# Recurrence, compression and attention of one mixer in another order (fp32 block pair, one core)

## What is computed

```python
def mixer_ab(h, w_in, conv_w, conv_b, w_r, b_r, w_i, b_i, lam, pe_k, pe_v, wk1, wk2, wv1, wv2, w_out):
    xr, gr, q, kc, vc, ks, vs, kw, vw, gl = jnp.split(h @ w_in, splits, axis=-1)
    y_rnn = rg_lru(causal_dwconv(xr, conv_w, conv_b), w_r, b_r, w_i, b_i, lam) * jax.nn.gelu(gr)
    y_att = nsa(q, kc, vc, ks, vs, kw, vw, gl, pe_k, pe_v, wk1, wk2, wv1, wv2)
    return jnp.concatenate([y_rnn, y_att], axis=-1) @ w_out
# rg_lru:  r, i = sigmoid(x @ w_r + b_r), sigmoid(x @ w_i + b_i)     (block diagonal)
#          log_a = -8 r softplus(-lam);  h_t = exp(log_a) h_{t-1} + sqrt(-expm1(2 log_a)) (i x)
```

## Time and profile before

| | us |
|---|---|
| median of three runs | 2596.81 |
| the profiled execution | 2601.1 |
| its span in the trace | 2597.6 |
| TensorE busy | 2420.9 (93%) |
| VectorE busy | 1654.0 (64%) |
| ScalarE busy | 1183.4 (46%) |
| mean granted TensorE clock | 0.93 of 2.4 GHz |

### The profile page before, as it was taken

How to read it: one execution, slowest core, us unless ns; L and a number is a source line. 1 busy time by engine, 2 the same in 40 slices (tenths; PEclk the granted TensorE clock), 3 DMA queues, 4 the chain that set the end, 5 groups by cost and what they waited for, 6 DMA issues and landing times.

```text
span 2597.6 us, 47292 instructions
## 1 busy us (share of the span) xinstructions
PE 2420.9 (93%) x18874; PEld 2299.5 (89%) x18874; DVE 1654.0 (64%) x2637; ACT 1183.4 (46%) x1720; POOL 50.7 (2%) x100
## 2 busy tenths in 40 slices
PE   7999999989997999999989999897799899897997
PEld 7999989879996999989978998797677799797997
DVE  5556889655554555888846555576543676666766
ACT  5444434544443444443544444344243456444654
POOL 0000000000001000000000000000000000000000
PEclk9999999989998999999989999896655899998999
DMA  6556454346556556545245555452200355353552
GB/s 250 179 185 223 150 177 137 110 157 212 185 179 202 186 185 200 194 146 173 97 141 190 192 182 198 159 162 74 81 1 9 111 181 186 114 179 99 186 185 96
DMA packets 110420, 405.90 MB, mean 156 GB/s; under 512 B 12256, under 2 KB 12384, under 8 KB 109920
## 3 DMA queue, kind: packets, MB, share of 16 engines
q1 hardware_dynamic: 96192, 352.33, 40.4%
q0 software_dynamic: 13824, 50.34, 5.6%
q10 hardware_dynamic: 288, 1.57, 0.2%
HBM read 403.14 MB, written 1.05 MB: 156 GB/s over the span
## 4 chain that ended last, share of the span: by engine, by line
PE 87%; DVE 8%; DMA 2%; ACT 2%; issue 1%; POOL 0%; DVEq 0%; SPq 0%; ACTq 0%
PE bank L482 85%; DMA mod_w_buf<-mod_w 2%; PE bank L622 2%; DVE w_lo L1349 1%; DVE arena L1509 1%; DVE work L1418 1%; DVE arena L1756 0%; ACT w_hi L1010 0%; DVE rinv L1383 0%; DVE work L1386 0%; ACT work L1169 0%; DVE rinv L1415 0%; POOL mod_w_buf L471 0%; DVE h_lo L1377 0%; ACT rinv L1031 0%
## 5 line engine op out<-in xcount | busy, mean ns | idle before, releaser
L482 PE MATMUL bank<-h_hi,w_hi 128*128 128x256 f32 (+1 forms) x4016 | 1172.3, 293 | 66.6 <-DVE h_lo L1644 18.2
L482 PE MATMUL bank<-h_hi,w_lo 128*128 128x256 f32 (+1 forms) x4016 | 1152.7, 288 | 0.0
L482 PE MATMUL bank<-h_lo,w_hi 128*128 128x256 f32 (+1 forms) x4016 | 1121.7, 285 | 0.0
L1349 DVE TENSOR_TENSOR w_lo<-w_raw,w_hi 128x1024 fp32r<-128x1024 f32 x663 | 809.2, 1223 | 488.5 <-ACT w_hi L1010 488.2
L1010 ACT ACTIVATE w_hi<-w_raw 128x1024 fp32r<-128x1024 f32 x663 | 699.2, 1056 | 734.1 <-PE bank L482 728.5
L482 PEld LDWEIGHTS bank<-h_hi,w_hi 128*128 128x128 f32 x4016 | 791.9, 197 | 95.5 <-issue 48.5
L482 PEld LDWEIGHTS bank<-h_hi,w_lo 128*128 128x128 f32 x4016 | 791.8, 197 | 0.0
L482 PEld LDWEIGHTS bank<-h_lo,w_hi 128*128 128x128 f32 x4016 | 771.0, 195 | 4.4 <-issue 4.3
L482 PE MATMUL bank<-hid_hi,w_hi 128*128 128x256 f32 x1056 | 299.2, 283 | 2.3 <-DVE hid_lo L1434 2.3
L482 PE MATMUL bank<-hid_lo,w_hi 128*128 128x256 f32 x1056 | 298.8, 283 | 0.0
L482 PE MATMUL bank<-hid_hi,w_lo 128*128 128x256 f32 x1056 | 298.8, 283 | 0.0
(11 more groups left out here) (205 smaller groups left out, 1857.1 us busy)
## 6 DMA issues: line engine op xcount, KB each, us to landing
w_raw<-weights SPq DMA_DIRECT2D x663, 512.0 KB, 3.3
mod_w_buf<-mod_w POOLq DMA_DIRECT2D x96, 512.0 KB, 4.9
tabs<-shape_tables SPq DMA_DIRECT2D x1, 1748.0 KB, 15.8
work<-v_bias ACTq DMA_DIRECT2D x2, 768.0 KB, 4.4
x<-x_fm SPq DMA_DIRECT2D x1, 1024.0 KB, 4.7
out_fm<-x SPq DMA_DIRECT2D x1, 1024.0 KB, 3.9
vecs<-vectors SPq DMA_DIRECT2D x1, 712.0 KB, 7.5
tabs<-shape_tables SPq DMA_DIRECT2D x1, 65.0 KB, 4.7
```

What stands on the lines that cost most here:

```text
L482: ins = pe.matmul(o, lhs, rhs, start=start, stop=stop, skip_group_check=share)
L1349: v.tensor_tensor(w_lo[:, n % SPLIT, :], w_raw[:, n % RAW, :], w_hi[:, n % SPLIT, :].bitcast(F32), ALU.subtract).then_inc(lo_ready[n % SPL ...
```

## The change

Memory: the operands of the r and i gates move to the two-slot buffers `hid_hi` and `hid_lo` (made larger), as does the compression operand, one kind at a time. The attention's buffers move to `kcs` and to the buffer of the first block's modulation weights. The steps `a_exp` and `amp` take the place of `den` and of the square root in `work`.

```diff
+RNN_UNITS = (10, 12, 14, 16, 18, 20, 22, 24)
...
-pct = work_row[:, 0:512]
-scc = work_row[:, 512:512 + NSA_HEADS * N_CMP].rearrange("p (a b) -> p a b", a=NSA_HEADS)
...
+amp = gg
+pt2 = mod_w_row[:, 0:1024].rearrange("p (a b) -> p a b", a=2)
...
 rtmp = work_row[:, 1024:2048].rearrange("p (a b) -> p a b", a=2)
-y2t = it.rearrange("p a b -> p (a b)").rearrange("p (a b) -> p a b", a=TT)
```

```diff
-for i in range(2):
-    column_pair()
-    q_rotated(2 + i)
+column_pair()
+q_rotated(2)
+column_pair()
+q_rotated(3)
 pe.wait_ge(kcs_ready, w.next(kcs_ready))
-for i in range(4):
-    column_pair()
-    if i == 1:
-        k_rotated(0)
-    if i == 3:
-        pe.wait_ge(kr_ready, w.next(kr_ready))
-        k_rotated(1)
-for i in range(2):
-    token_pair()
-branch_gates()
-pe.wait_ge(xc_ready, w.next(xc_ready))
 r_slot = slot()
 i_slot = slot()
 for m in range(KT):
     b = pair_bank()
-    product(half(b, 0), r_slot, m, h_hi[:, m, :], h_lo[:, m, :], True, True)
-    product(half(b, 1), i_slot, m, h_hi[:, m, :], h_lo[:, m, :], True, True, pair_full)
+    pe.wait_ge(xc_ready, w.next(xc_ready))
+    product(half(b, 0), r_slot, m, hid_hi[:, m % 2, :], hid_lo[:, m % 2, :], True, True)
+    if m == KT - 1:
+        slot_done()
+    product(half(b, 1), i_slot, m, hid_hi[:, m % 2, :], hid_lo[:, m % 2, :], True, True, pair_full)
+    if m == KT // 2:
+        k_rotated(0)
 slot_done()
-pe.wait_ge(kcs_split, w.next(kcs_split))
-b = pair_bank(hv_ready)
+branch_gates()
+pe.wait_ge(kr_ready, w.next(kr_ready))
+k_rotated(1)
+for i in range(2):
+    token_pair()
+pe.wait_ge(kr_ready, w.next(kr_ready))
 for kind in range(2):
+    pe.wait_ge(kcs_split, w.next(kcs_split))
     for t in range(2):
         n = slot()
         at = kind * SEQ + t * NSA_KV
...
+            product(bank[3][:, at:at + (N_CMP + 1) * NSA_KV], n, k,
+                    op_hi[:, :, pairs].rearrange("p g n -> p n g"),
+                    op_lo[:, :, pairs].rearrange("p g n -> p n g"),
+                    (kind, t, k) == (0, 0, 0), last, cmp_sum_full if last else None, share=True)
         slot_done()
+    column_pair()
...
-for i in range(KT // 2):
-    column_pair(yrnn_ready if i == 0 else None)
...
+    column_pair()
     pe.wait_ge(cp_ready, w.next(cp_ready))
...
         scores(u)
+    if u in RNN_UNITS:
+        k = RNN_UNITS.index(u)
+        if k % 2 == 0:
+            rnn_bank = pair_bank()
+        column(half(rnn_bank, k % 2), None if k else yrnn_ready, pair_full if k % 2 else None)
     if 1 <= u <= nsa_units:
         turns(u - 1)
```

```diff
+xc_high(0)
+xc_high(1)
 state["tile"] += 1
 for m in range(KT):
     b, free = next_pair(0)
+    if m + 2 < KT:
+        xc_high(m + 2)
     act_f(th[:, m, :], half(b, 0), ACT.Sigmoid, bias=vec("b_r", 0, m)).then_inc(act_link, 1)
...
+operand_high(0)
+b, free = next_pair(1)
+act_f(glog, two(bank[b][:, :])[:, :, 0:3 * NSA_HEADS], ACT.Sigmoid).then_inc(free, 1)
 act.wait_ge(act_link, w.next(act_link, KT))
 act.wait_ge(decay_ready, w.next(decay_ready))
+high_parts(state["tile"] + 2)
+for m in range(KT):
+    ins = act_f(a_exp[:, m, :], th[:, m, :], ACT.Exp, scale=tiny[:, 0, m:m + 1])
+ins.then_inc(act_link, 1)
+b, free = next_pair()
+act_f(vsw[:, 0, :, :], two(bank[b][:, :]), ACT.Copy).then_inc(free, 1)
+act.wait_ge(act_link, w.next(act_link))
 for m in range(KT):
     ins = act_f(th[:, m, :], th[:, m, :], ACT.Tanh, scale=decay[:, m:m + 1])
 ins.then_inc(th_ready, 1)
 act.wait_ge(th_ready, w.next(th_ready))
-act.wait_ge(kr_ready, w.next(kr_ready, 2))
+b, free = next_pair()
+act_f(vsw[:, 1, :, :], two(bank[b][:, :]), ACT.Copy).then_inc(free, 1)
+act_f(amp, th, ACT.Sqrt, scale=-1.0).then_inc(amp_ready, 1)
+state["tile"] += 1
 high_parts(state["tile"] + 1)
-act_f(work[:, :, :], th, ACT.Sqrt, scale=-4.0).then_inc(amp_ready, 1)
-b, _ = next_pair(4)
+state["tile"] += 1
+act.wait_ge(cmp_sum_full, w.next(cmp_sum_full))
+operand_high(1)
...
+gelu_input(0)
+state["tile"] += 1
+high_parts(state["tile"] + 1)
+state["tile"] += 1
+high_parts(state["tile"] + 1)
+act.wait_ge(cmp_sum_full, w.next(cmp_sum_full))
...
+gelu_input(1)
...
+    gelu_input(2 + qt, ACT.Gelu_apprx_tanh if qt else ACT.Copy)
...
+for i in range(0, KT - 2, 2):
+    act_f(gg[:, i:i + 2, :], gg[:, i:i + 2, :], ACT.Gelu_apprx_tanh).then_inc(gelu_ready, 1)
...
+    if 1 <= u <= KT // 2:
+        act.wait_ge(rnn_ready, w.next(rnn_ready))
+        k = 2 * (u - 1)
+        act_f(h_hi[:, k:k + 2, :], th[:, k:k + 2, :], ACT.Copy).then_inc(high_ready, 1)
+    if u in RNN_UNITS:
+        k = RNN_UNITS.index(u)
+        state["tile"] += 1
+        high_parts(state["tile"] + 1)
+        if k % 2:
+            b, free = next_pair(0)
+            act_f(yrnn_out[:, k - 1:k + 1, :], two(bank[b][:, :]), ACT.Copy).then_inc(free, 1)
```

```diff
+next(steps, None)
 v.memset(tiny[:, 7, :], 0.0).then_inc(xc_sum, 1)
-for kind in range(2):
-    skip_pairs(2)
+skip_pairs(1)
+rotate_q(2)
+skip_pairs(1)
+rotate_q(3)
...
+xc_low(0)
+xc_low(1)
+state["tile"] += 1
+for m in range(KT):
+    skip_pairs(1, 0)
+    if m + 2 < KT:
+        xc_low(m + 2)
+state["tile"] += 1
+rotate_k(0)
...
+operand_low(0)
+rotate_k(1)
+low_parts(state["tile"] + 2)
+dve.wait_ge(pair_full, w.last(pair_full))
+v.tensor_tensor(it, it, xc, ALU.mult).then_inc(dve_link, 1)
+skip_pairs(1)
 dve.wait_ge(th_ready, w.next(th_ready))
-v.tensor_scalar(den, th, -1.0, 1.0, ALU.mult, ALU.add).then_inc(dve_link, 1)
+v.scalar_tensor_tensor(a_exp, a_exp, 1.0, th, ALU.add, ALU.mult).then_inc(dve_link, 1)
+skip_pairs(1)
+dve.wait_ge(dve_link, w.next(dve_link, 2))
+v.tensor_scalar(a_exp, a_exp, 1.0, None, ALU.add).then_inc(dve_link, 1)
+low_parts(state["tile"] + 2)
+dve.wait_ge(amp_ready, w.next(amp_ready))
+v.tensor_tensor(it, it, amp, ALU.mult).then_inc(amp_used, 1)
+state["tile"] += 2
+low_parts(state["tile"])
 dve.wait_ge(dve_link, w.next(dve_link))
+dve.wait_ge(amp_used, w.next(amp_used))
+v.scalar_tensor_tensor(it, a_exp, 1.0, it, ALU.add, ALU.mult).then_inc(dve_link, 1)
+operand_low(1)
 low_parts(state["tile"] + 1)
-for i in range(0, KT, KT // 2):
-    v.reciprocal(den[:, i:i + KT // 2], den[:, i:i + KT // 2])
-    low_parts(state["tile"] + 2 + 2 * i // KT)
-v.tensor_tensor(it, it, xc, ALU.mult).then_inc(dve_link, 1)
+skip_pairs(1)
 dve.wait_ge(dve_link, w.next(dve_link))
-v.tensor_tensor(it, it, den, ALU.mult).then_inc(dve_link, 1)
-dve.wait_ge(dve_link, w.next(dve_link))
-dve.wait_ge(amp_ready, w.next(amp_ready))
-v.tensor_tensor(it, it, work[:, :, :], ALU.mult).then_inc(dve_link, 1)
-dve.wait_ge(dve_link, w.next(dve_link))
-v.scalar_tensor_tensor(th, th, 1.0, den, ALU.add, ALU.mult).then_inc(dve_link, 1)
-dve.wait_ge(dve_link, w.next(dve_link))
-for m in range(KT):
-    ins = v.tensor_tensor_scan(xc[:, m, :], th[:, m, :], it[:, m, :], 0.0, ALU.mult, ALU.add)
+for m in range(KT // 2):
+    v.tensor_tensor_scan(xc[:, m, :], a_exp[:, m, :], it[:, m, :], 0.0, ALU.mult, ALU.add)
+state["tile"] += 2
+low_parts(state["tile"] + 1)
+for m in range(KT // 2, KT):
+    ins = v.tensor_tensor_scan(xc[:, m, :], a_exp[:, m, :], it[:, m, :], 0.0, ALU.mult, ALU.add)
 ins.then_inc(dve_link, 1)
...
+skip_pairs(1)
...
+    skip_pairs(1)
...
-    v.scalar_tensor_tensor(s, bank[u % 2][:, 0:2 * length].rearrange("p (b k) -> p b k", b=2), SCALE,
-                           rows(tab(f"causal{qt}"), 2), ALU.mult, ALU.add).then_inc(sc_free, 1)
-    dve.wait_ge(sc_free, w.next(sc_free))
-    v.tensor_reduce(nmax[:, 2 * u:2 * u + 2], s, X_AXIS, ALU.max, negate=True).then_inc(smax, 1)
+    for br in range(2):
+        v.tensor_tensor_reduce(s[:, br], bank[u % 2][:, br * length:(br + 1) * length],
+                               tab(f"causal{qt}"), -SCALE, -4.0 * NEG, ALU.add, ALU.min,
+                               nmax[:, 2 * u + br:2 * u + br + 1]).then_inc(sc_taken, 1)
+    if u < KT // 2:
+        if u < KT // 2 - 1:
+            dve.wait_ge(gelu_ready, w.next(gelu_ready))
+        v.tensor_tensor(th[:, 2 * u:2 * u + 2, :], xc[:, 2 * u:2 * u + 2, :], gg[:, 2 * u:2 * u + 2, :],
+                        ALU.mult).then_inc(rnn_ready, 1)
...
+        dve.wait_ge(rnn_ready, w.next(rnn_ready))
+        for kt in (k, k + 1):
+            v.tensor_tensor(h_lo[:, kt, :], th[:, kt, :], h_hi[:, kt, :].bitcast(F32), ALU.subtract
+                            ).then_inc(yrnn_ready, 1)
+    if u in RNN_UNITS:
+        advance(1)
```

```diff
-for name in ("kc", "vc", "xr", "q", "ks", "kw", "gr"):
+for name in ("kc", "vc", "xr", "q", "ks", "kw"):
...
-for name in ("cmp_wk1_2", "cmp_wv1_2"):
-    add(a[name][0].reshape(2, KT, P, P).transpose(0, 2, 1, 3))
+gl = np.zeros((D_MODEL, P), w.dtype)
+gl[:, :3 * NSA_HEADS] = at["gl"]
+add(block_tiles(gl))
+add(token_tiles(at["vs"]))
+add(token_tiles(at["vw"]))
+gr = block_tiles(at["gr"])
+add(a["cmp_wk1_2"][0].reshape(2, KT, P, P).transpose(0, 2, 1, 3))
+add(gr[0:2])
+add(a["cmp_wv1_2"][0].reshape(2, KT, P, P).transpose(0, 2, 1, 3))
```

(46 more changed lines are left out.)

115 lines of the change are left out of this document (54 added, 61 removed).

## The result

The changed kernel takes 2530.26 us (median of four executions, 2526.87 to 2537.69), the kernel before on the same chip 2597.94. The ratio is 0.9738, 95% interval [0.9719, 0.9757]: 68 us less. The forecast was 2526 with a range of 2498 to 2575. The profiled execution took 2527.78 us.

What follows compares the result with a forecast made beforehand. TensorE, busy 93% of the span, bounds the kernel; only its idle and low-clock time can go. Stage 55, attention 15 and last columns 1 make 71 off 2601.1: 2530, less 4.3 to the median, 2526 us; range 2498 to 2575.

Steps and rivals of the forecast that it cites:

- The stage: From the end of the kw columns to the first attention score: 106 us against 161.4, 55 less.
- Waits: TensorE's waits that remain or arise in the stage, (a) to (g): 18 us in sum.
- (a): At r and i: TensorE waits for `xc_low(0)`, queued behind the last query rotation, 2.5 us.
- (g): At the stage's end: the first attention scores wait for the last compressed output as now, 1.5 us.
- (c): ScalarE's exponentials, tanhs and table load precede weight splits; first low split of compression weights behind a 2.3 us pass: 3.
- (d): Second gr column's low part stands behind another 2.3 us pass and the second operand's split: 2.5 us.
- (e): Copies for TensorE stand behind a low split that ScalarE frees only after two Gelus with table load: 3.5 us.
- (f): Compressed scores: the pair's copy, then a Gelu table load, stand before the turned probabilities' copy: 4 us.
- (b): r and i loop: ScalarE's three short instructions per tile outlast TensorE's work, but key rotation fills it: 1 us.
- The clock: In the stage: four low-clock spells at 2 us each (8) and three ramps (7), 15 us in sum.
- The attention: 32 units with all eight columns inside; first column lifts the clock from unit 10 on: 15 us less.
- the second (clock down in the attention): Rival: the attention's clock stays at 1.2 GHz, 56 us worse, 2582 us; chance 0.13.

Runs made afterwards that it cites:

- experiment 1: Changed kernel with its eight recurrence output columns in one block behind the attention's 32 units: 2567.12 us, ratio 0.9877.
- experiment 3: Changed kernel with the old two-step score instructions (scale and mask, then maximum) in place of the new one: 2543.74 us, ratio 0.9791.
- experiments 4 and 5: 4: kernel before with only new coefficients, 2587.97 us; with only output columns moved into attention, 2577.24. 5: changed kernel with two unused reciprocals added, 2540.02.
- experiments 2: Changed kernel with columns in units 10 to 17: 2552.84 us; that plus three unused matmuls in unit 19: 2530.20; columns in units 5, 7 to 19: 2522.22.
- experiment 7: Changed kernel with columns from unit 5 and unused matmuls in two gaps at the attention's start: 2514.83 us; also in the stage's other gaps: 2510.38.

## Why the prediction was right

**Sum.** The gain can be put down to three parts, two of them priced by a run. Leaving the columns out of the attention costs 37 (experiment 1), and 13.5 of that hang on the new score instruction too (experiment 3). VectorE's reciprocals cost 10 in either order (experiments 4 and 5). The remaining 21 of 68 is the order of the stage, by subtraction alone; no run isolates it.

**The stage** was put at 106 and took 107.5. TensorE's work of 73.3 at 2.4 GHz is confirmed within 4: at a mean of 0.81 the clock was low for some 41 of the 107.5 us, nearly all of them busy, which is some 20 us of loss in the 96.2 of busy time and leaves 76. VectorE was put at some 60 and is busy for 61.2. **Waits** were put at 18 and are 11.3 (107.5 less 96.2). Term (a) was 2.5 and is 2.5, and (g) is 1.5. Term (c), 3, is 1.6: it was the chain of eight tanhs, a pass of 2.29 and a low part, without a table load in front of the tanhs. Terms (d) and (e), 6 together, didn't come, but 1.7 for the compressed keys and values (L1859), which no term named, did. Term (f), 4, is 1.5, twice 0.74: a Gelu with its table load does stand ahead of the second of these copies, but the load is over (1824.97) before the Gelu's input is there, and TensorE waits no longer than for the first copy, which has none. Term (b), 1, is 2.6, and it is the one that was missed: not three short instructions but the sigmoid's table load (1.28 in the chain), behind a weight split of 1.06, which makes 2.1 of the 2.6. **The clock** was put at 15 and cost about 20. The spells foreseen are there (the 48-column gates at 1744, the two compressions at 1768 and 1785, the compressed scores at 1802 and 1815), but the first compression's is 10.5 us long, and one more came at 1727, between the two waits at the gates (the records lengthen from 1727.07 on, and the second wait starts after that). Charging 2 us and a ramp for each was the term that was too small. Waits 7 less, clock 5 more and work 3 more nearly cancel: that the stage came out within 2 us is partly luck.

**The attention** was put 15 below its 118.1 and is 15.4 below. Units 0 to 9 stayed at 1.2 GHz but for the first 3 us, as taken, and the first column lifted the clock within 3 us. Units of the first half without a column take 1.34 to 1.49 where I had 1.7, and those of the second 2.48 (the distance of the first block's loop, 2.50) where I had 2.33.

**What was right for an incomplete reason.** I took the first block's rows as proof that the loop holds the clock. It holds it but can't raise it: the units alone, with TensorE as well covered, ran at 0.51 over 111 us in experiment 1, and units without a column kept 1.00 in experiments 2 and 7. The forecast of the attention stood on there being no gap of a microsecond or more behind the last column, and it didn't ask for one: at most 0.48 us in the changed kernel until 0.85 in the last unit, 1.24 and 1.47 in experiments 2 and 3, which is 22.6 and 13.5 us of time. That the chosen units kept it short was luck. I also put the new score instruction's worth at nothing beyond its own time, and it was 13.5. Of the rivals, the second (clock down in the attention) is what experiment 1 brings about.

The Trainium skill (TensorE: Matmul & The Clock Gate, Part 4: PE-mode transpose) says of a transpose that "it doesn't count as PE-busy the same way", so that the full clock doesn't engage for it. The runs are consistent with it as far as raising goes, since the units never lift the clock by themselves, but units with four transposes each hold it, as the window of experiment 7 shows. No run here separates the transposes from the 64-column matmuls beside them.

**The end.** The microsecond from the last output columns didn't come: the stretch is 33.3 us in both kernels. TensorE waits 2.4 and 1.4 us at its start, and in the changed kernel the clock falls there from 1.00 to 0.50, from 1932 to 1942. The kernel before came in at 0.50 and rose at 2010, 8 us into the stretch, so the means are alike (0.86 and 0.87).

## What to carry to other kernels

Where TensorE is covered and yet slow, ask first which idle stretch took the clock away and which wide work could bring it back; here a few dense columns at the start and no gap of a microsecond behind them did it. Where no useful work was at hand, three matmuls that nobody reads were worth 22 us in the kernel with its columns in a row, and six at the attention's start 7 in a better one. Judge a shorter chain on another engine by the gap that it prevents, not by its own duration. And read a busy share of 57% on VectorE by place: at the place of the recurrence it had no slack, and 13 us put back came out as 10.
